# Attention steps: where the first half's normalisation stands among the maxima, and how many weight tiles an MLA head splits

## The reference, cut to what matters

```python
# fox, per head, causal
s = q @ k.T * Dh**-0.5 + F[:, None] - F[None, :]
p = softmax(where(kpos <= qpos, s, -inf));  o = p @ v

# MLA: c_q is 384 wide (3 tiles of 128), c_kv is 256 wide (2 tiles of 128)
q  = (rmsnorm(c_q, q_norm) @ w_q_b).reshape(B, S, 16, 64 + 32)
kv = (rmsnorm(c_kv, kv_norm) @ w_kv_b).reshape(B, S, 16, 64 + 64)
s  = (q_nope @ k_nope.T + q_rope @ k_rope.T) * 96**-0.5     # masked by chunk
o  = softmax(s) @ v
y  = (o.reshape(B, S, 1024) * silu(z)) @ w_out
```

## Time and profile before

| | us |
|---|---|
| median of 3 runs | 2225.04 (2224.86 to 2226.74) |
| the profiled execution | 2225.34 |
| its span, first to last instruction | 2223.5 |
| PE busy | 2064.3 (93%) |
| DVE / POOL / ACT busy | 1109.1 / 1095.0 / 673.4 |

### The profile page before, as it was taken

How to read it: one execution, slowest core, us unless ns; L and a number is a source line. 1 busy time by engine, 2 the same in 40 slices (tenths; PEclk the granted TensorE clock), 3 DMA queues, 4 the chain that set the end, 5 groups by cost and what they waited for, 6 DMA issues and landing times.

```text
span 2223.5 us, 26435 instructions
## 1 busy us (share of the span) xinstructions
PE 2064.3 (93%) x9488; PEld 1657.0 (75%) x9488; DVE 1109.1 (50%) x1189; ACT 673.4 (30%) x1085; POOL 1095.0 (49%) x651
## 2 busy tenths in 40 slices
PE   5999999989999999999999998997999999989996
PEld 3777767877788788788878876886777777768774
DVE  6545556465631212112111278314888888863576
ACT  3345564222221000000000032112666666650312
POOL 1545555414734633633443373334666666654373
PEclk9999999989999999999999998997999999989997
DMA  3100001103211211211111121111000000001122
GB/s 136 49 20 20 19 10 38 38 29 117 83 47 47 76 47 47 77 46 50 63 53 51 48 95 47 48 49 38 19 21 19 19 19 19 19 29 47 48 76 95
DMA packets 31641, 106.64 MB, mean 48 GB/s; under 512 B 3449, under 2 KB 3641, under 8 KB 31577
## 3 DMA queue, kind: packets, MB, share of 16 engines
q1 hardware_dynamic: 27520, 96.14, 13.1%
q10 hardware_dynamic: 4066, 9.74, 1.2%
HBM read 101.51 MB, written 4.26 MB: 48 GB/s over the span
## 4 chain that ended last, share of the span: by engine, by line
PE 66%; POOL 10%; DVE 10%; issue 10%; ACT 3%; ACTq 0%; DMA 0%; POOLq 0%; DVEq 0%
PE ps L225 49%; POOL probs_lo L684 7%; PE ps L390 4%; PE ps L242 3%; PE ps L254 2%; POOL w_lo L1938 2%; POOL w_hi L1936 1%; DVE h_lo L371 1%; PE ps L628 1%; DVE tmp L1764 1%; DVE x L1766 1%; PE ps L635 1%; DVE S_all L1296 1%; PE ps L629 1%; PE ps L616 1%
## 5 line engine op out<-in xcount | busy, mean ns | idle before, releaser
L1936 POOL TENSOR_TENSOR w_hi<-w_raw,zero 128x1024 fp32r<-128x1024 f32 (+1 forms) x173 | 333.9, 1930 | 820.6 <-PE ps L225 579.5
L1938 POOL TENSOR_TENSOR w_lo<-w_raw,w_hi 128x1024 fp32r<-128x1024 f32 (+1 forms) x173 | 432.9, 2502 | 13.6
L225 PE MATMUL ps<-h_hi,w_lo 128*128 128x512 f32 x1328 | 334.8, 394 | 5.3 <-DVE x L517 5.1
L225 PE MATMUL ps<-h_hi,w_hi 128*128 128x512 f32 x1328 | 328.0, 389 | 0.0
L225 PE MATMUL ps<-h_lo,w_hi 128*128 128x512 f32 x1216 | 300.4, 389 | 0.0
L225 PEld LDWEIGHTS ps<-h_hi,w_lo 128*128 128x128 f32 x1328 | 249.4, 189 | 60.3 <-issue 9.3
L684 POOL TENSOR_TENSOR probs_lo<-probs,mla_p_hi 128x512 fp32r<-128x512 f32 x192 | 218.2, 1158 | 150.2 <-ACT probs L677 150.2
L225 PEld LDWEIGHTS ps<-h_hi,w_hi 128*128 128x128 f32 x1328 | 249.2, 188 | 51.8
L225 PEld LDWEIGHTS ps<-h_lo,w_hi 128*128 128x128 f32 x1216 | 228.4, 188 | 47.7
L1378 DVE TENSOR_TENSOR tmp<-ps,tmp 128x1024 f32<-128x1024 f32 x22 | 26.9, 1224 | 370.3 <-PE ps L225 363.6
L719 DVE TENSOR_REDUCE mx<-ps 128x1 f32<-128x128 f32 (+1 forms) x192 | 137.4, 751 | 79.8 <-PE ps L660 48.9
(11 more groups left out here) (341 smaller groups left out, 3738.4 us busy)
## 6 DMA issues: line engine op xcount, KB each, us to landing
w_raw<-in_wpack SPq DMA_DIRECT2D x173, 512.0 KB, 3.2
x<-in_xT ACTq DMA_DIRECT2D x16, 512.0 KB, 7.9
out<-result SPq DMA_DIRECT2D x8, 512.0 KB, 2.9
p_raw<-in_pT ACTq DMA_DIRECT2D x1, 1024.0 KB, 6.8
pos_i<-in_pos SPq DMA_DIRECT2D x1, 512.0 KB, 6.4
const_stage<-in_consts SPq DMA_DIRECT2D x1, 404.0 KB, 3.5
vec<-in_vecs SPq DMA_DIRECT2D x1, 284.0 KB, 4.4
mla_q_hi<-c_neg ACTq DMA_DIRECT2D x16, 4.0 KB
```

What stands on the lines that cost most here:

```text
L225: last = nc.tensor.matmul(dst[:, half, :], w[slot][:, kt, :], a[:, i, t], start=(n == 0), stop=(n == total - 1))
L1936: nc.gpsimd.tensor_tensor(w_hi[s][:, kts, :], raw[s][:, kts, :], no_change[:, kts, :], ALU.add).then_inc(w_hi_done, 1)
L1938: nc.gpsimd.tensor_tensor(w_lo[s][:, kts, :], raw[s][:, kts, :], w_hi[s][:, kts, :].bitcast(F32), ALU.subtract)\
```

## The change

The diff makes two changes. First, `norm_half_dve` of half 0 is issued behind the sixth maximum (`NORM_AFTER = 5`) instead of behind the fourth, in the steps of both attentions. Second, in the MLA steps POOL splits only tiles 0 to 4 of a head's unit; the last step splits all eight, since the unit it prepares is the first of the output projection. For that the last pair of steps is written out behind POOL's loop, for fox too, where all units keep eight tiles.

```diff
+        NORM_AFTER = 5
@@ step_dve
             for i in range(N_MAX):
                 max_dve(dve, A, n, i)
-                if i == 3 and prev is not None:
+                if i == NORM_AFTER and prev is not None:
                     norm_half_dve(dve, A, prev, 1 - b, 0, tile, gate)
@@
+        MLA_KTS = (QL + KVL) // P
@@ gpsimd
-            def heads(A, first):
-
-                def step(n, b, turn):
+            def heads(A, first, kts):
+
+                def step(n, b, turn, k=slice(0, kts)):
                     u = first + b + 1
-                    split(turn * 2 + u, u % 2, turn * 16 + (u // 2 * 16 + 16))
+                    split(turn * 2 + u, u % 2, turn * 16 + (u // 2 * 16 + 16), k)
                     if not (isinstance(n, int) and n == 0):
                         for g in range(N_PIECES):
                             low_pool(pool, A, n - 1, g)
-                steps(pool, A, step)
+                last = A.heads // 2 - 1
+                for b in range(2):
+                    step(b, b, 0)
+                with pool.Fori(1, last) as turn:
+                    for b in range(2):
+                        step(turn * 2 + b, b, turn)
+                step(2 * last, 0, last)
+                step(2 * last + 1, 1, last, slice(0, DT))
                 for g in range(N_PIECES):
                     low_pool(pool, A, A.heads - 1, g)
@@
-            heads(fox, U_FQK)
+            heads(fox, U_FQK, DT)
@@
-            heads(mla, U_HEAD)
+            heads(mla, U_HEAD, MLA_KTS)
```

## The result

The changed kernel takes 2259.06 us (median of 4 runs, 2258.25 to 2259.78) against 2225.31 for the kernel before: 1.0156 times the time before, 95% interval 1.0143 to 1.0168. The forecast was slower by 0.4%, 2234.6 us in a range of 2224 to 2245. The sign was right, and the size too small by 24.5 us.

What follows compares the result with a forecast made beforehand. The prediction took PE, busy 93% of the span, as the bound. Fox 7 x 0.90 = +6.3 and MLA 15 x 0.66 - 14 x 0.47 = +3.3 gave +9.6 us: 2234.6 us, range 2224 to 2245.

Steps and rivals of the forecast that it cites:

- What PE waits for: Expected profile: wait before block 6 gone from MLA; new waits before turned values and row of maxima, 1.5 us MLA, 1 fox.
- MLA tail: End of each MLA step: the moved normalisation delays the eighth maximum, so the row of maxima starts 0.66 us later.
- the frame of the prediction: Timestamps of the MLA step before the change: row of maxima starts at 1632.94, forecast to move to 1633.60.
- its 0.6: MLA tail: time allowed for POOL's piece 10, from 1629.56 to 1630.16, before the normalisation's L712 could finish.
- The early rope addition: MLA steps 2 to 15: L1687 on DVE starts before POOL's piece 0, gaining 0.47 us a step, bounds 0 and 0.66.
- Fox, +0.90 us a step: Fox tail: eighth maximum ends later, row of maxima starts 0.90 us later in 7 steps, +6.3 us; bounds 0.8 to 1.5.
- The sum: Whole kernel: fox +6.3 and MLA +3.3 give +9.6 us, forecast 2234.6 us against the median, 0.4% slower.
- rival 3: MLA and fox tails: L708 and L712 both blocked behind whole POOL pieces, +26 us, 2251 us; chance 0.06.
- The pair of steps written out behind POOL's loop: POOL's program: added instructions might cause a fetch hiccup; taken as 0, bounds 0 to 2 us in all.

## Why the prediction was wrong

- **What PE waits for.** Right for the waits that count. The wait before block 6 went, and a wait before L647 and L670 came. Not foreseen was the 0.48 us for POOL's last piece just before it. Beside the moved normalisation POOL's piece 10 takes 1.20 us and the last, piece 11, 0.90. The wait for the maxima behind it ends later, so by itself it costs nothing.
- **MLA tail, +0.66 us a step.** Right. Of the step at 1611, DVE in the kernel after:

```profile
1607.65 0.96 DVE L722 TENSOR_REDUCE mx<-ps 128x1 f32<-128x768 f32 x1 [0.80 <-PE ps L663]
1608.64 0.69 DVE L708 TENSOR_TENSOR newton<-ps,r 64x512 f32<-64x512 f32 x1
1609.37 0.83 DVE L711 SCALAR_TENSOR_TENSOR rec<-newton,r 64x512 f32<-64x512 f32 x1
1610.38 0.97 DVE L715 TENSOR_TENSOR rec<-rec,mix 64x512 f32<-64x512 f32 x1 [0.18 <-DVE rec L711]
1611.38 0.69 DVE L717 SCALAR_TENSOR_TENSOR mix<-ps,rec 64x512 f32 x1
1612.10 2.22 DVE L722 TENSOR_REDUCE mx<-ps 128x1 f32<-128x896 f32 x2
```

  Block 5 ends 19.36 us earlier than in the frame of the prediction; shifted by that, L717 was forecast to end at 1612.04 (measured 1612.07) and the eighth maximum at 1614.19 (1614.32). Both waits for POOL, 0.83 for 0.69 and 0.97 for 0.69, are those that the sum placed. One term is not what its row says: the sum gives piece 10 "its 0.6", and the row that it names has 0.73, with which L717 would have ended 0.13 us later. POOL's piece ended 0.60 us behind L711, so the figure came out right by luck.
- **The early rope addition, 0.47 us in each of 14 steps, shared by both edits.** Mechanism right: with the short split alone it gave 0.35 us a step, where 0.34 was forecast. Beside the moved normalisation it was not measured by itself. A step at full clock took 27.1 us in the changed kernel, and 26.9 and 27.4 in turn, 27.2 on average, in the kernel with five filling matmuls, for the 27.05 forecast. So tail and gain together were 0.2 us a step too favourable at most.
- **Fox, +0.90 us a step, 6.3 in all.** Mechanism right, size too small: 1.2 us a step. Fox steps are of two kinds. Before, they took 28.7 and 29.0 us in turn, and the sum was worked out on one of the shorter kind. At full clock they take 29.7 and 30.4 us in the kernel after, 1.0 and 1.3 more. From the mask of block 5 to L670 the two kinds lose 0.97 and 1.13 us; and behind the shorter kind PE starts the next projection 0.23 us later than before:

```profile
268.18 0.27 PE L670 MATMUL ps<-ident,mx 128*8 128x128 f32 x1 [0.26 <-DVE mx L722]
268.65 0.72 PE L225 MATMUL ps<-h_hi,w_lo 128*128 128x512 f32 x2 [0.20 <-issue]
```

  That makes about 8.3 of the 10.3 us, and it is what the filled kernel shows, where the clock did not fall in steps 2 to 7 of fox: 210.93 - 202.65 = 8.3 us. The other 2 go with the clock: one fall of 3.4 us in the last fox step, which took 31.3 us, and a lower clock in the first, 0.93 for 0.96.
- **"The sum."** This is the step that failed. It priced PE's waits by their length and took every duration from rows at a granted clock of 1.00. The price of a wait is its length and what the clock does behind it. In MLA that second term was about 21 us, more than twice the whole forecast. It was not among the rivals either: rival 3 gave 2251 us by longer blocking, a mechanism that did not occur. With the waits filled the same kernel takes 2237.5 us, 3 us above the forecast: the rest of the sum held to that. The Trainium skill, "TensorE: Matmul & The Clock Gate", Part 1, ties the clock to how busy PE has just been; the two filled kernels agree with that, by their 0.99 for 0.92 over MLA.
- **The pair of steps written out behind POOL's loop.** Taken at 0, and nothing speaks against it: the short split alone, which has it too, came out 1.3 us below its expectation.

## What to carry to other kernels

When an edit moves an engine's block of work past a wait, list that engine's later instructions with their new ends, and look for gaps in front of them: the engine that is busy for only half of its time overall can still be the one that ends the step. Mixing the block into the gaps paid 13 us, moving it whole cost 40. When TensorE gets new waits, even of about 1 us, price a fall of its clock as well, and test it cheaply by filling the wait with matmuls of no use. Whether it matters that two waits lie close together, or only how much PE stands idle, these runs don't separate. And a hidden instruction is not free if it holds what another engine's visible instruction needs.

## What the runs showed of the hardware

- PE's clock fell in this kernel behind waits that are short: 0.48 and 1.20 us with one short matmul between, in steps that are busy for 24.7 of 27.1 us. It was then granted 0.50 for 6.8 us. With the second wait shortened to at most 0.7 us it fell once in the stretch instead of 13 times, and a wait of 1.14 us elsewhere in the step had not made it fall.
- Two matmuls of no use in a step, which shortened the wait from 1.2 to 0.7 us, were worth as much as five: 21 us over 15 steps.
- The falls came in a pattern that the program does not have: of three steps with the same instructions, one ran at 1.00, one at 0.88 and one at 0.94, and from the sixth step on they take 29.5 and 28.5 us in turn. The pattern is the same, to 0.2 us from the first row of maxima, in the changed kernel and in those with the move alone and with the move in MLA alone.
